# Eight weight slots instead of six in overlaid buffers, one gate table, and scatter columns made per expert group

## What is computed

```python
def _expert_choice_ffn(u, w_router, w_g, w_u, w_d):
    cap = CAPACITY_FACTOR * n // N_EXPERTS                 # 32 tokens for each of 16 experts
    aff = jax.nn.softmax(jnp.einsum('bnd,de->ben', u, w_router), axis=1)
    gate, idx = lax.top_k(aff, cap)
    xe = u[bidx, idx]
    ye = (silu(xe @ w_g) * (xe @ w_u)) @ w_d * gate        # per expert, all 1024 x 1024
    return jnp.zeros_like(u).at[bidx, idx].add(ye)
...
for layer in range(DEPTH):                                 # DEPTH = 2
    m_lat = _modulation(cond_lat, w_mod[layer], b_mod[layer])    # 1024 x 6144
    y_lat = mixer(_modulate(h_lat, m_lat[0], m_lat[1]))
    h_lat = _post_norm(h_lat, m_lat[2] * y_lat, ...)
    f_lat = _expert_choice_ffn(_modulate(h_lat, m_lat[3], m_lat[4]), ...)
    h_lat = _post_norm(h_lat, m_lat[5] * f_lat, ...)
```

## Time and profile before

| | us |
|---|---|
| median of 3 runs | 2275.27 (2272.72 to 2278.9) |
| profiled execution | 2275.23 |
| its span, first to last instruction | 2273.4 |
| TensorE busy (matmuls) | 1796.1 (79%) |
| DVE busy | 529.6 (23%) |
| ScalarE busy | 363.2 (16%) |
| POOL busy | 59.3 (3%) |
| weights and all else read | 584.09 MB, 257 GB/s over the span |

### The profile page before, as it was taken

How to read it: one execution, slowest core, us unless ns; L and a number is a source line. 1 busy time by engine, 2 the same in 40 slices (tenths; PEclk the granted TensorE clock), 3 DMA queues, 4 the chain that set the end, 5 groups by cost and what they waited for, 6 DMA issues and landing times. The chain is left out here.

```text
span 2273.4 us, 27624 instructions
## 1 busy us (share of the span) xinstructions
PE 1796.1 (79%) x11960; PEld 1059.1 (47%) x11960; DVE 529.6 (23%) x1051; ACT 363.2 (16%) x729; POOL 59.3 (3%) x69
## 2 busy tenths in 40 slices
PE   6897665656568977565655559999999999999999
PEld 4454121212116742111111137877578678785785
DVE  1434000100003231000000034342343233414432
ACT  1231000000001010000000012233331022324310
POOL 0000000000000000000000000120000001100000
PEclk9997788887789987878888779999999999999999
DMA  9692999999997466999999943221322332112221
GB/s 405 247 408 74 421 428 428 429 428 429 427 428 312 177 267 291 428 428 429 428 428 423 428 203 149 76 76 61 146 81 107 121 148 75 71 61 111 111 83 47
DMA packets 43502, 586.54 MB, mean 258 GB/s; under 512 B 4912, under 2 KB 5040, under 8 KB 8080
## 3 DMA queue, kind: packets, MB, share of 16 engines
q1 hardware_dynamic: 40464, 574.11, 61.2%
q0 software_dynamic: 2224, 8.31, 0.9%
q10 hardware_dynamic: 720, 2.74, 0.3%
HBM read 584.09 MB, written 1.05 MB: 257 GB/s over the span
## 5 line engine op out<-in xcount | busy, mean ns | idle before, releaser
L1316 PE MATMUL ps<-ring,arena 128*32 128x512 f32 x2048 | 328.3, 776 | 228.1 <-DMA ring<-in_experts 215.6
L1316 PEld LDWEIGHTS ps<-ring,arena 128*32 128x32 f32 x2048 | 64.8, 127 | 481.1 <-DMA ring<-in_experts 334.8
L1082 PE MATMUL ps<-arena,ring 128*128 128x256 f32 (+3 forms) x1344 | 272.1, 364 | 10.5 <-issue 3.2
L1316 PE MATMUL ps<-arena 128*32 128x512 f32 x1024 | 168.4, 793 | 113.5 <-DMA arena<-in_experts 113.4
L1082 PEld LDWEIGHTS ps<-arena,ring 128*128 128x128 f32 (+2 forms) x1344 | 234.2, 190 | 46.7 <-issue 6.0
L1413 PE MATMUL ps<-arena,ring 128*128 128x256 f32 x768 | 183.4, 388 | 0.0
L1413 PEld LDWEIGHTS ps<-arena,ring 128*128 128x128 f32 x768 | 142.8, 191 | 29.5 <-issue 10.0
L1436 PE MATMUL ps<-arena,ring 128*128 128x256 f32 x640 | 147.7, 381 | 0.0
L1316 PEld LDWEIGHTS ps<-arena 128*32 128x32 f32 x1024 | 33.4, 128 | 238.2 <-DMA arena<-in_experts 160.0
L2061 DVE TENSOR_TENSOR arena<-ps,arena 128x512 f32<-128x512 f32 x16 | 10.3, 687 | 535.5 <-PE ps L1316 535.5
L1436 PEld LDWEIGHTS ps<-arena,ring 128*128 128x128 f32 x640 | 120.7, 190 | 25.8 <-issue 10.1
(11 more groups left out here) (330 smaller groups left out, 1910.6 us busy)
## 6 DMA issues: line engine op xcount, KB each, us to landing
ring<-in_experts SPq DMA_DIRECT2D x128, 2048.0 KB, 26.0
ring<-in_stream SPq DMA_DIRECT2D x66, 2048.0 KB, 8.7
arena<-in_experts SPq DMA_DIRECT2D x64, 2048.0 KB, 25.7
arena<-in_stream SPq DMA_DIRECT2D x10, 2048.0 KB, 12.4
ring<-in_stream SPq DMA_DIRECT2D x2, 1696.0 KB, 7.1
ring<-in_stream SPq DMA_DIRECT2D x4, 512.0 KB, 3.8
tab<-in_tables_first SPq DMA_DIRECT2D x1, 1729.0 KB, 24.5
ring<-in_stream SPq DMA_DIRECT2D x2, 768.0 KB, 4.4
```

Of the source, the lines that this page charges most:

```text
L1082: mm = M(dst, lhs(k), rhs(k), start=k == 0, stop=k == n - 1)
L1316: mm = M(bank(b + half)[32 * e:32 * e + 32], x[:, k, 32 * e:32 * e + 32], wk[:, e, half * HALF:(half + 1) * HALF], start=k == 0, stop=k == ...
```

## The change

The widened ring has eight slots: four in the ring tensor, and four in `arena` from column `EXTRA` = 7840 on, each of 8 x 512 columns (before, 8 x 520). Six of them (0 to 3, 6 and 7) are used from the first chunk on; slots 4 and 5 share their columns with the mixer's inputs and norm scratch, and are used from chunk ("mod", 0, 11) on, behind the same two waits as before. At block two the four ring slots are taken in the order in which they came free.

To make room, buffers with different lifetimes lie over each other: the norm's `t` over the experts' sums, the convolution's `conv` and `mix` over its `c`, the pooled values over the attention's probabilities, the router's matrices over the experts' buffers, and `part` half in `small` and half in `arena`. Layer 1's gates go into layer 0's table: POOL loads each half of its bias when `post_norm` has used that half last. `put` for all experts is gone: DVE makes the scatter matrix of one group in each turn of the loop, from two columns that POOL copies to `cols_g`; TensorE no longer waits for POOL before the scatter. The second block's tables, which overwrite the iota table, now wait for the scatter matrix of the last turn.

```diff
-WIDE = 6
+WIDE = 8
+EARLY = (0, 1, 2, 3, 6, 7)
-SLOT = 8 * 520
+SLOT = 8 * HALF
@@ two_block_program
-    widened = number[("mod", 0, 6)] + 1
+    widened = number[("mod", 0, 11)]
+    early = len(EARLY)
+    wide = [s for s in range(WIDE) if s not in EARLY] + [EARLY[(widened + i) % early] for i in range(early)]
     for n, (key, _) in enumerate(order):
         if n < widened:
-            place.append(n % RING)
+            place.append(EARLY[n % early])
         elif n < narrowed:
-            place.append((4, 5, 2, 3, 0, 1)[(n - widened) % WIDE])
+            place.append(wide[(n - widened) % WIDE])
         else:
-            place.append((n - narrowed) % RING)
+            if n == narrowed:
+                narrow = sorted(range(RING), key=lambda s: latest[s])
+            place.append(narrow[(n - narrowed) % RING])
...
-        EXTRA = 12980
+        EXTRA = 7840
...
@@ SyncE
-                elif place[n] >= RING:
+                elif n >= widened:
                     sp.wait_ge(*consumed(("mix_in", 2)))
...
@@ TensorE, behind the 24 chunks of a turn
                     pe.wait_ge(*Svx.turn(g, "ye"))
-                    pe.wait_ge(*Spl.turn(g, "put"))
@@ DVE, gates
-                if j == 4:
-                    ve.wait_ge(*loaded(f"gate_bias{l}", 2))
+                if j % 6 == 4:
+                    ve.wait_ge(*loaded(f"gate_bias{j // 6}", l + 1))
...
@@ DVE, router and loop
-                V.tensor_copy(ff["cols"], bank(1, 8)).then_inc(*Sv.up("cols", l))
-                ve.wait_ge(*Sv.at("cols", l))
-                for g in range(NG):
-                    V.tensor_scalar(ff["put"][:, g], T2("iota"), ff["cols"][:, g:g + 1], ff["cols"][:, 4 + g:5 + g],
-                                    ALU.is_equal, ALU.mult).then_inc(*Sv.up("put", l, g))
+                V.tensor_copy(ff["cols"], bank(1, 8).rearrange("p (c g) -> p c g", c=2)).then_inc(*Sv.up("cols", l))
...
+                    ve.wait_ge(*Spl.turn(g, "cols"))
+                    V.tensor_scalar(ff["put_g"], T2("iota"), ff["cols_g"][:, 0], ff["cols_g"][:, 1], ALU.is_equal, ALU.mult
+                                    ).then_inc(*Sx.up("put"))
                     ve.wait_ge(used, g * (3 * KD) + (base + 2 * KD))
@@ POOL
-            def gate_bias(l):
+            def gate_bias(l, i):
+                m = (2, 5)[i]
+                if l:
+                    po.wait_ge(*S("post_dve").at("weighed", 0, i, 1, 1))
...
-                    po.wait_ge(*S("ffn_dve").at("put", l, 3))
+                    po.wait_ge(*S("ffn_dve").at("cols", l))
                     po.wait_ge(used, g * (3 * KD) + (base + 1))
-                    G.tensor_copy(ff["put_g"], ff["put"][:, bass.ds(g, 1)].rearrange("p a n -> p (a n)")).then_inc(*Sx.up("put"))
+                    G.tensor_copy(ff["cols_g"], ff["cols"][:, :, bass.ds(g, 1)]).then_inc(*Sx.up("cols"))
...
-                    po.wait_ge(*S("ffn_dve").at("put", 1, 3))
+                    po.wait_ge(*S("expert1_dve").turn(NG - 1, "put"))
...
-            gate_bias(0)
+            gate_bias(0, 0)
+            gate_bias(0, 1)
             po.wait_ge(*consumed(("mod", 0, 7)))
-            gate_bias(1)
             ln_params(0, 0, None)
             router(0)
+            gate_bias(1, 0)
             ffn(0)
             ln_params(0, 1, S("post_dve").at("h", 0, 0, 1))
+            gate_bias(1, 1)
             ln_params(1, 0, S("post_dve").at("h", 0, 1, 1))
```

More of the change, by code:

```diff
@@ L412, in two_block_program @@
         sc = Scratch()
-        m0 = dict(mix=sc.take(2048, KD), pt=sc.take(1024, TT), q=sc.take(1024, 4), k=sc.take(512), v=sc.take(512, 4),
-                  prob=sc.take(1024, 2), prob_t=sc.take(1024, 2), stat=sc.take(64), pooled=sc.take(1024, 4),
-                  ut=sc.take(2048, KD), uc=sc.take(2048, KD))
+        m0 = dict(mix=sc.take(2048, KD), pt=sc.take(1024, TT), q=sc.take(1024, 4), k=sc.take(512), v=sc.take(512, 4))
+        m0["pooled"] = Scratch(sc.top).take(1024, 4)
+        m0.update(prob=sc.take(1024, 2), prob_t=sc.take(1024, 2), stat=sc.take(64))
@@ L416, in two_block_program @@
+        parts = (small_t[:, 640:1152], sc.take(512))
         assert sc.top <= EXTRA, sc.top
         sc = Scratch(EXTRA)
+        m0.update(ut=sc.take(2048, KD), uc=sc.take(2048, KD))
         m0.update(sq=sc.take(512), sd=sc.take(512), xn=sc.take(512), t1=sc.take(512), t2=sc.take(512))
+        assert sc.top <= EXTRA + 2 * SLOT, sc.top
         sc = Scratch()
-        m1 = dict(ut=sc.take(2048, KD), c=sc.take(2048, KD), z=sc.take(KD * 258, KD), conv=sc.take(2048, KD),
-                  mix=sc.take(2048, KD))
+        m1 = dict(c=sc.take(2048, KD), z=sc.take(KD * 258, KD), ut=sc.take(2048, KD))
@@ L422, in two_block_program @@
+        m1["conv"] = m1["mix"] = m1["c"]
         sc = Scratch()
[L423 to L426, removed]
+        ff = dict(xg=sc.take(1024, KD), hg=sc.take(1024), acc=sc.take(2048, TT), ht=sc.take(1024, KD), ye=sc.take(1024),
+                  pick=sc.take(1024, TT), pick_g=sc.take(256, TT), put_g=sc.take(256), vals=sc.take(32), ex=sc.take(32, TT),
+                  st=sc.take(16), idf=sc.take(32), cols=sc.take(8, 2), cols_g=sc.take(2, 2))
@@ L427, in two_block_program @@
+        pn = dict(t=ff["acc"], st=sc.take(24, TT), mv=sc.take(4, TT), rs=sc.take(4, TT))
+        assert sc.top <= EXTRA, sc.top
+        ff.update(wk=Scratch().take(256), di=Scratch(1024).take(512, E), dg=Scratch(1536).take(512, E), ut=Scratch(4096).take(2048, KD))
         idx_u = ctx.enter_context(nc.sbuf_tensor("idx", [P, CAP], U32))
-        sc = Scratch(21300)
-        md = dict(part=sc.take(1024, 2), condT=sc.take(256, KD), sig=sc.take(16))
+        sc = Scratch(EXTRA + (WIDE - RING) * SLOT)
@@ L431, in two_block_program @@
+        md = dict(condT=sc.take(256, KD), sig=sc.take(16))
         modcol_t = sb("modcol", 128)
         modcol = modcol_t[:, :].rearrange("p (l m k c) -> p l m k c", l=2, m=4, k=KD)
[L433 to L436, removed]
-        pn = dict(t=sc.take(2048, TT), st=sc.take(24, TT), mv=sc.take(4, TT), rs=sc.take(4, TT))
         MOD_BANKS = {"front": (0, 3), "mixer": (4, 4), "attention": (0, 0), "early": (2, 3), "late": (6, 6)}
@@ L1020, in mod_fold @@
                 g, _ = mod_place((l, j))
-                part = md["part"][:, mod_half((l, j))]
+                part = parts[mod_half((l, j))]
                 pe.wait_ge(*S("mod_act").at("part", l, j))
@@ L1956, in post_norm @@
                         y = ff["acc"][:, a, cols] if part else bank(2 * a + half)
-                        V.tensor_tensor(t, y, gates[l][:, part, cols], ALU.mult).then_inc(*Sv.up("weighed", *k))
+                        V.tensor_tensor(t, y, gate[:, part, cols], ALU.mult).then_inc(*Sv.up("weighed", *k))
                         ve.wait_ge(*Sv.at("weighed", *k))
@@ L2414, in _ @@
             G = nc.gpsimd
-            def gate_bias(l):
-                for i, m in enumerate((2, 5)):
-                    po.dma_start(gates[l][:, i], w["b_mod"][l:l + 1, m * D:(m + 1) * D].to_broadcast([P, D])
-                                 ).then_inc(loaded(f"gate_bias{l}")[0], 16)
+            def gate_bias(l, i):
+                m = (2, 5)[i]
+                if l:
+                    po.wait_ge(*S("post_dve").at("weighed", 0, i, 1, 1))
+                po.dma_start(gate[:, i], w["b_mod"][l:l + 1, m * D:(m + 1) * D].to_broadcast([P, D])
+                             ).then_inc(loaded(f"gate_bias{i}")[0], 16)
             def ln_params(l, part, last):
```

8 lines of the change are left out of this document (4 added, 4 removed).

## The result

The changed kernel takes 2255.95 us (median of four runs, 2253.9 to 2256.91) against 2276.47 us for the kernel before in the same series: a ratio of 0.9913, interval 0.9900 to 0.9926, some 20 us or 0.9%. The forecast was 2254.8 us. The profiled execution took 2256.84 us, with a span of 2255.0 us and again 1.8 us around it.

The account below looks back on a forecast made before the run. DMA engines set the two expert loops (904 us), TensorE and the chains around it the other 1370 us. Span 2273.4 - 9.79 - 9.79 - 0.89 = 2252.9, with 1.8 us around it 2254.8 us; range 2247 to 2265.

Parts of the forecast that it names:

- Eight slots, layer 0: Layer 0's expert loop: two extra chunks landed before it starts, so its stream ends 9.79 us earlier.
- Eight slots, layer 1: Layer 1's expert loop: releases shift by two chunks in the same way, 9.79 us again.
- The output projection: Convolution's output projection between the loops: the wait for its second weight chunk goes, gain 0.89 us.
- Early slots: Mixer, six slots instead of four: no weight is late there, gain 0; bounds under 1.6 us gain, 2 us loss.
- scatter columns: Router and expert turns: DVE's operations leave the router, one per turn behind POOL's small copy; gain 0, 6.4 us if uncovered.
- gate table: Two gate loads moved past layer 0's last uses, outside the continuous streams: cost 0; 2.4 us if both fell inside.
- overlays: Overlaid buffers: same operations and shapes, no added wait; 0, give or take 0.5 us.
- The second block: After the loops: its first TensorE work waits for DVE, not weights, so it moves up whole.
- One head start lost: One loop's 9.79 us is given back by transfer order or TensorE falling behind; 2264.6 us, chance 0.06.
- No effect: Expert loops: no more than six chunks stand ahead, so streams begin as now; 2275 us, chance 0.04.
- A slower stream: Both loops: chunks take longer than 4.897 us with the new slot places; 2298 us at 5% more, chance 0.04.
- the waits inside the loops go too: Expert loops: more buffers fill the gap before each chunk, removing 329.0 us; 1946 us, chance 0.01.

Follow-up runs that it names:

- e1: Changed kernel, but SyncE may run only six chunks ahead in both expert loops; 2272.46 us, 0.9994 of the kernel before.
- e2: Changed kernel, but SyncE may run only seven chunks ahead in both expert loops; 2266.28 us, 0.9967 of the kernel before.
- e3: Changed kernel, but only six chunks ahead in layer 0's expert loop, eight in layer 1's; 2264.51 us, 0.9959 of the kernel before.
- e4: Changed kernel with four slots instead of six before the loops' ring is widened; 2254.55 us, 0.9919 of the kernel before.
- e9: Changed kernel unaltered, run again on one chip beside e10; 2255.01 us, 0.9914 of the kernel before.
- e6: Kernel before with only the one gate table and its four separate loads; 2276.26 us, 1.0010 of the kernel before.
- e5: Kernel before with only the scatter matrices made per expert group, in each turn; 2275.37 us, 1.0009 of the kernel before.
- e7: Changed kernel with all loads POOL issues inside the expert loops (second norms' parameters, second block's loads) moved ahead of them; 2248.87 us, 0.9889 of the kernel before.
- e10: The version of e7 run again beside the changed kernel on one chip; 2248.17 us, 0.9880 of the kernel before.
- e8: Changed kernel with only the second norms' parameter loads moved ahead of the expert loops; 2253.16 us, 0.9910 of the kernel before.

## Why the prediction was right

The sum was 2254.8 us; the profiled execution took 2256.84 us and the median is 2255.95 us. Step by step, by the prediction's own marks:

**Eight slots, layer 0.** Forecast 9.79 us, measured 9.86 us (449.69 to 439.83). The issue that waits for TensorE is the ninth, as it said. e1, e2 and e3 show that depth alone does it.

**Eight slots, layer 1.** Forecast 9.79 us, measured 9.23 us. e3, e4 and e9, of the same depth in this loop, measured 9.4 to 9.7 us. The term had the right size.

**The output projection.** Forecast 0.89 us, and here the mechanism is not borne out: the prediction took the wait of one execution for one of the kernel. The changed kernel starts these instructions at 793.77 with no wait for a landing, and the stage between the loops is 0.73 us shorter. But with six slots the wait is missing too in e6, as its first row of the projection shows, and in e5 (at 807.10):

```profile
803.61 7.10 PE L1082 MATMUL ps<-arena 128*128 128x512 f32 x16
```

Their stage takes 192.28 and 192.31 us, against 191.90 to 192.16 in the changed kernel, e1, e3, e4 and e9, which have eight slots there and end loop 0 alike. So 0.1 to 0.4 us lie between six and eight slots, and no run shows what they are; the rest of the 0.73 us goes with the wait in the one profile of before.

**Early slots, scatter columns, gate table, overlays.** All were put at 0, with bounds of a few us on either side. e4, e5 and e6 keep the first three inside the interval of the runs. The bound of the small copy was 0 to 0.40 us and 0.40 was taken: it took 0.19 us. The overlays were tried only together with the rest, in e1: 2272.46 against 2274.42 us, a ratio whose interval holds 1. So no loss is to be seen in them, and no gain is shown.

**The second block.** It was to move up whole. From the last chunk to the end it took 954.0 us against 953.2 us, of which 0.57 us are the last chunk itself (3.37 against 2.80 us).

**What is left of the difference.** The median lies 1.2 us from the sum. That close a match is luck, since the changed kernel's own runs lie between 2252.6 and 2260.3 us (e9); the size of the two loop terms is not. Against the forecast span of 2252.9 us the profile is 2.1 us over: +0.68 at the first chunk, -0.07 in loop 0, +0.16 between, +0.56 in loop 1, +0.74 after it. The first and the last are within what these columns spread over the other kernels (222.5 to 228.9, and 950.8 to 954.8); the 0.56 us is 0.1 to 0.4 us in e3, e4 and e9 (443.60, 443.64, 443.87).

**The rivals.** One head start lost (2264.6 us) is what e3 was built to give, at 2264.51 us, and the changed kernel is 8.6 us below it. No effect (2275 us) is what e1 gives, at 2272.46 us against 2274.42 for the kernel before. A slower stream is refuted by the pace: (664.95 - 635.55) / 6 = 4.90 us a chunk after, 4.897 before, with ring and arena slots mixed. That the waits inside the loops go too is refuted by the 313.9 us that stay of 329.0. The profile page's section on DMA issues adds why depth cannot help there:

```profile
ring<-in_experts SPq DMA_DIRECT2D x96, 2048.0 KB, 35.8
arena<-in_experts SPq DMA_DIRECT2D x96, 2048.0 KB, 35.7
```

A chunk now takes 35.8 us from issue to landing, where it took 25.7 to 26.0 us with six slots (the same section of before). The two more chunks in the queue, 9.8 us, are simply waited for longer: within a saturated stream a deeper queue is latency, not rate.

**What the prediction did not price.** It charged 2.4 us for two gate loads if they fell into a stream, and found that they didn't. Of the second block's tables it said that they "still share the stream, as now", without a price, and the norm parameters in both loops it did not name. These loads cost the changed kernel 9.5 to 9.9 us of its loops (e7, e10). Both kernels issue them there, so the forecast was untouched. But it is half of the 19.1 us that the change took from the loops, and of the whole time e7's order of POOL's program takes another 6.8 us (e10 against e9), a third of what the change brought.

## What to carry to other kernels

When a loop is bound by its transfers (share 1.00, equal steps of bytes over rate), an extra slot is worth one transfer for each time the loop is entered after an idle stretch of the DMA engines (4.3 to 5.2 us here, for a transfer of 4.9), and nothing inside the loop: count the entries, check that the idle stretch holds the extra transfers, and multiply. Then list every issue of the other queues that falls inside the loop, because each of their bytes lengthened it here at about the same rate; what is not needed until after the loop and has room before it belongs before it. Book the result stage by stage between fixed marks, since one execution's start moves more than a small edit brings.

## What the runs showed of the hardware

**The start varies by 6 us, and the granted clock with it.** e9 and e8 have the same program on every engine until POOL issues e8's norm loads at 198.75, but the first expert chunk starts at 222.53 us in e9 and at 228.88 us in e8. They ran on two chips; e6, on e8's chip, starts at 225.09. The stretches of e9:

```profile
16.00:36.00 20.00, 14.67 (x102) 7.68 (x95) 2.10 (x8) 4.93 (x9) 1.23 (x2) 0.91 1.01 423
36.00:90.00 54.00, 52.35 (x236) 35.17 (x234) 21.18 (x23) 8.51 (x14) 0.00 (x0) 0.97 0.92 373
90.00:125.00 35.00, 29.41 (x234) 14.54 (x234) 12.96 (x32) 13.97 (x34) 1.58 (x3) 1.00 1.01 426
125.00:193.00 68.00, 60.42 (x334) 33.23 (x330) 27.93 (x60) 16.21 (x37) 0.53 (x1) 1.00 0.66 269
```

and of e8:

```profile
16.00:36.00 20.00, 14.45 (x97) 7.37 (x89) 2.41 (x9) 4.54 (x9) 1.23 (x2) 0.81 1.00 423
36.00:90.00 54.00, 53.10 (x230) 36.79 (x234) 20.26 (x22) 7.52 (x12) 0.00 (x0) 0.94 0.89 353
90.00:125.00 35.00, 28.88 (x222) 12.76 (x211) 11.85 (x29) 13.26 (x29) 1.58 (x3) 0.95 1.00 421
125.00:193.00 68.00, 63.63 (x350) 34.84 (x344) 24.22 (x56) 16.76 (x38) 0.00 (x0) 0.97 0.62 259
```

The granted clock was 0.91, 0.97, 1.00 and 1.00 in e9, and 0.81, 0.94, 0.95 and 0.97 in e8. The clock that e8 lacks, each difference times the length of its stretch, comes to 2.0 + 1.6 + 1.8 + 2.0 = 7.4 us by this estimate, less where TensorE sat idle, against a start that is 6.35 us later: the size fits. e5, another kernel, has e8's four values (0.81, 0.94, 0.95, 0.97) and starts at 228.80. Why the clock was granted lower in these executions is not shown. Nor is how much of the spread between runs of one kernel it explains: two runs of the kernel before in e5's series took 2271.11 and 2281.05 us at the same mean clock of 0.899.

**The end of a loop varies by 1.7 us, and not by chance alone.** TensorE's last chunk of a loop (16 matmuls) takes 1.92 us in some profiles and up to 3.64 us in others. The stretches of the last chunk of loop 0, first e9's and then e10's:

```profile
662.54:664.46 1.92, 1.92 (x16) 0.41 (x16) 0.00 (x0) 0.00 (x0) 0.00 (x0) 1.00 1.00 427
```

```profile
662.54:666.07 3.53, 3.52 (x16) 0.59 (x16) 0.00 (x0) 0.00 (x0) 0.00 (x0) 0.52 1.03 436
```

The granted clock is 1.00 in the one and 0.52 in the other; with 1.2 and 2.4 GHz as the two levels, the longer time is near twice the shorter. The wait ahead differs too: 1.65 us in e9, 2.98 us in e10. In the 24 loop ends of the twelve profiles, all ten quick last chunks (1.92 or 1.93 us) follow a wait of 1.3 to 1.7 us, and twelve of the fourteen slow ones (2.76 to 3.64 us) a wait of 2.96 to 2.98 us. A long wait is what a quick chunk leaves of the step (1.92 + 2.98 = 4.90), so quick and slow chunks tend to follow each other, and what counts is which kind the last one is. In loop 0 that went by the kernel: slow in e2, e7, e8 and e10, quick in the eight others. Why is open, but by it the stage between the loops is some 1.7 us longer in these four (193.8 to 194.6 us). Inside the loop a slow chunk costs nothing, since 3.64 us is still under 4.90 us; at the loop's end it goes into the time.

**One core held 426 GB/s for 440 us,** with transfers of 2048 KB, in a program that runs on this core alone. The Trainium skill (DMA: Bandwidth & Descriptors, Bandwidth) has 425 GB/s for one large transfer and says that the figure is for a core whose neighbour is idle; the loops' rows agree. The 358 GB/s that the prediction set against the trace belong, by that section, to two cores streaming at once, which no run here shows.
